# Rounded parts for the latent up-projections, index scores grouped by width, paired score blocks, and a two-piece load of x in a kernel of two transformer blocks

## The reference

```python
q = (_rmsnorm(cq, qa_g) @ w_uq).reshape(B, S, H, MLA_NOPE + MLA_ROPE)
kv = (_rmsnorm(ckv, kva_g) @ w_ukv).reshape(B, S, H, MLA_NOPE + MLA_V)
...
score = jax.nn.relu(jnp.einsum('bqhd,bkd->bqhk', qi, kidx).astype(jnp.float32))
index = jnp.einsum('bqh,bqhk->bqk', wi, score) * idx_scale
```

## Time and profile before

| | |
|---|---|
| three runs | 1757.21, 1757.62, 1757.74 us; median 1757.62 |
| the profiled execution | 1759.74 us, of which the span from the first to the last instruction is 1757.9 |
| granted TensorE clock, mean | 0.998 |
| PE busy | 1749.2 us of the span |
| DVE, ACT, POOL busy | 1032.4, 757.8, 421.5 us |

### The profile page before, as it was taken

The page is one execution under the profiler, slowest core; times in us unless marked ns, Lnnn a source line. Parts: engine busy times, 40 slices in busy tenths (PEclk is TensorE's granted clock), DMA queues, the critical chain, the costliest instruction groups (busy, mean ns, idle before and its releaser), DMA issues.

```text
span 1757.9 us, 25383 instructions
## 1 busy us (share of the span) xinstructions
PE 1749.2 (100%) x9298; PEld 1435.9 (82%) x9298; DVE 1032.4 (59%) x2170; ACT 757.8 (43%) x1396; POOL 421.5 (24%) x326
## 2 busy tenths in 40 slices
PE   9999999999999999999999999999999999999998
PEld 7778878777887888888888888889888888888887
DVE  4888776688877665555433455445756655555333
ACT  6466644546564523233233455556434322222222
POOL 4545553454644500000000332330200200000000
PEclk9999999999999999999999999999999999999999
DMA  6432123323212343333333422223322333333332
GB/s 192 129 100 73 49 65 93 96 68 105 73 49 73 103 132 96 98 96 98 102 108 103 155 61 84 85 84 109 96 73 61 91 100 97 95 95 95 102 103 94
DMA packets 54421, 166.18 MB, mean 95 GB/s; under 512 B 10200, under 2 KB 10712, under 8 KB 54328
## 3 DMA queue, kind: packets, MB, share of 16 engines
q1 hardware_dynamic: 53032, 162.12, 30.6%
q10 hardware_dynamic: 1296, 2.84, 0.5%
HBM read 162.25 MB, written 2.17 MB: 94 GB/s over the span
## 4 chain that ended last, share of the span: by engine, by line
PE 99%; DMA 0%; DVE 0%; ACT 0%; ACTq 0%; POOL 0%; issue 0%; DVEq 0%
PE proj L1113 80%; PE turned L1427 2%; PE o L1449 2%; PE proj L1591 1%; PE proj L1584 1%; PE o L1692 1%; PE o L1792 1%; PE score L1397 1%; PE turned L1079 1%; PE turned L1671 1%; PE score L1781 1%; PE proj L1301 1%; PE turned L1654 1%; PE score L1386 1%; PE score L1654 0%; PE score L1269 0%
## 5 line engine op out<-in xcount | busy, mean ns | idle before, releaser
L1113 PE MATMUL proj<-hhi,whi 128*128 128x512 f32 x1456 | 582.6, 400 | 0.0
L1113 PE MATMUL proj<-hhi,wlo 128*128 128x512 f32 x1456 | 568.4, 390 | 0.0
L1113 PE MATMUL proj<-hlo,whi 128*128 128x512 f32 x1456 | 567.4, 390 | 0.0
L1876 ACT ACTIVATE whi<-ring 128x1024 fp32r<-128x1024 f32 x279 | 295.4, 1059 | 623.7 <-PE proj L1113 602.3
L2384 DVE TENSOR_TENSOR wlo<-ring,whi 128x1024 fp32r<-128x1024 f32 x199 | 243.2, 1222 | 161.2 <-ACT whi L1876 160.7
L1113 PEld LDWEIGHTS proj<-hhi,whi 128*128 128x128 f32 x1456 | 274.0, 188 | 63.6 <-issue 10.4
L1113 PEld LDWEIGHTS proj<-hhi,wlo 128*128 128x128 f32 x1456 | 273.4, 188 | 58.6
L1113 PEld LDWEIGHTS proj<-hlo,whi 128*128 128x128 f32 x1456 | 274.1, 188 | 53.5 <-issue 0.7
L839 POOL TENSOR_TENSOR wlo<-ring,whi 128x512 fp32r<-128x512 f32 x160 | 215.5, 1369 | 339.9 <-ACT whi L1876 339.9
L857 POOL TENSOR_TENSOR prob<-prob 128x512 f32<-128x512 f32 x36 | 56.9, 1581 | 872.2 <-ACT prob L1872 872.2
L1902 ACT ACTIVATE prob<-prob,negmax 128x256 f32<-128x256 f32 (+3 forms) x208 | 114.0, 550 | 74.1 <-DVE negmax L2457 73.4
(11 more groups left out here) (379 smaller groups left out, 2436.9 us busy)
## 6 DMA issues: line engine op xcount, KB each, us to landing
ring<-wstream SPq DMA_DIRECT2D x285, 512.0 KB, 3.6
arena<-lines SPq DMA_DIRECT2D x28, 256.0 KB, 5.7
arena<-x ACTq DMA_DIRECT2D x4, 512.0 KB, 6.3
out<-arena SPq DMA_DIRECT2D x8, 256.0 KB, 2.9
arena<-mem SPq DMA_DIRECT2D x1, 1024.0 KB, 8.5
ring<-wstream SPq DMA_DIRECT2D x12, 64.0 KB, 2.2
ring<-wstream ACTq DMA_DIRECT2D x2, 256.0 KB, 7.7
arena<-rope SPq DMA_DIRECT2D x4, 128.0 KB, 6.4
```

Of the source, the lines that this page charges most:

```text
L1113: mm = pe.matmul(b, rounded(w), rounded(rhs(v, k)), start=(first and n == 0 and p == 0), stop=(last and n == len(blocks) - 1 and p == 2))
L1876: act.activation(rounded(dst), src, ACT.Copy, scale=scale).then_inc(ready, 1)
```

## The change

1. **Up-projections from rounded parts.** UK, UV and UQ become three products of rounded parts like all the others. New work to make the parts: ACT makes high parts of `ckvn`, of the UK and UV weights, of `cqn` (all ahead of `prepare_after("VT0")`), and of the UQ weights (after step 1's exponentials); DVE makes low parts of `ckvn`, UK and UV after `stage_v(0)`; POOL makes the two low parts of `cqn` ahead of the `kA` additions, and those of UQ after UV1. In `TAKE`, UK and UV move ahead of BK1, which goes from slot 11 to slot 13.
2. **Index scores by width.** The four units of a group now have one query block: two groups of 512 columns, two of 384, two of 256. On DVE each accumulation then waits for the one just before it.
3. **C's scores of two blocks at once.** C takes its blocks in the order 0, 2, 3, 1. At steps 24 and 28, `scores` does this step's (128 columns) and the next one's (384) in the same two banks; at steps 25 and 29 it does nothing. `PLAN` moves by a few chunks from step 24 on.
4. **Setup.** x comes in two column pieces of four token parts each; SP issues those of tokens 0 and 2 and slots 0 and 1, ACT those of tokens 1 and 3. Eight warm-up products at first and four more in `first_job`; the four high·high products of the first column piece come ahead of the transposes of the second. The squares of x are summed in two halves; POOL, not ACT, makes slot 1's high part, and the spread of the norm factors comes two chunks later in `second_job`.

The diff, cut to its core:

```diff
-WARM = 12
-X_ORDER = (1, 2, 3, 4, 5, 6, 7, 0)
+WARM = 8
+X_ORDER = (1, 2, 3, 0, 4, 5, 6, 7)
-TAKE = (... "VT0", "BQ1", "BK1", "UK", "UV", "VT1", "UQ", ...
+TAKE = (... "VT0", "BQ1", "UK", "UV", "BK1", "VT1", "UQ", ...
+C_ORDER = (0, 2, 3, 1)
+def double_step(s):
+    return C_STEP <= s < STEPS and s % 4 == 0
 def idx_unit(n):
-    return 4 * (n // (4 * (NQB - 1))) + n % 4, n % (NQB - 1) + 1
+    return n % 8, NQB - 1 - n // 8
...
+            sp.dma_start(ident[:, :], ident_in).then_inc(ident_loaded, 16)
+            for tok in (0, 2):
+                load_x(sp, 0, tok)
+            load_w0(0, w0_loaded)
+            for tok in (0, 2):
+                load_x(sp, 1, tok)
+            load_w0(1, wload[0])
+            sp.dma_start(ring[:, 1, :], wstream[TAKE_FROM[1]]).then_inc(wload[1], 16)
... (pool)
                 after_low(SLOT_OF["BK1"])
                 pool.wait_ge(relu_ready, L * IDX_UNITS + IDX_UNITS)
+                pool.wait_ge(up_out, L * LAYER_UP + 4)
+                for k in range(2):
+                    pool.tensor_tensor(rounded(cqn_lo[:, k, :]), cqn[:, k, :], cqn_hi[:, k, :], ALU.subtract).then_inc(kA_ready, 1)
+                pool.wait_ge(kA_ready, L * LAYER_KA + 2)
                 for h in range(4):
                     pool.tensor_tensor(kA[rows, h, :], krope[rows, 0, :], krope[rows, 1, :], ALU.add).then_inc(kA_ready, 1)
...
                         prepare_after(name)
+                        if name == "UV1":
+                            low_queries()
... (pe, first_job)
+                for _ in range(4):
+                    pe.matmul(b[:, 0:P], ones[:, :], ones[:, :], start=True, stop=True)
+                for n in range(NT):
+                    high_product(n)
                 for n in range(KC + LOW_LAG):
                     if n < KC:
                         k = X_ORDER[n]
+                        if n < NT:
+                            turn_x(1, n)
... (pe, up_k; up_v and up_q alike)
-                    pe.wait_ge(latent_ready, L * 3 + 3)
-                    pe.matmul(b[:, :], w[:, pair * P:(pair + 1) * P], ckvn, start=True, stop=True).then_inc(up_done, 1)
+                    pe.wait_ge(latent_ready, L * LAYER_LATENT + 5)
+                    for p, (w, v) in enumerate(((uk_hi[:, cols], ckvn_hi), (uk_hi[:, cols], ckvn_lo), (wlo[:, slot, cols], ckvn_hi))):
+                        mm = pe.matmul(b[:, :], rounded(w), rounded(v), start=(p == 0), stop=(p == 2))
... (pe, scores)
+                        for t in (s, s + 1) if double_step(s) else (s,):
+                            for p, (q_part, k_part) in enumerate(((q_hi, k_hi), (q_hi, k_lo), (q_lo, k_hi))):
+                                for b in range(2):
+                                    parts(t, b, q_part, k_part, p == 0, p == 2)
... (act)
+                act.wait_ge(latent_ready, L * LAYER_LATENT + 3)
+                high(ckvn, ckvn_hi, up_out)
+                high(raw_loaded("UK")[:, 0:2 * P], uk_hi, up_out)
+                high(raw_loaded("UV")[:, 0:2 * P], uv_hi, up_out)
+                high(cqn, cqn_hi, up_out)
                 prepare_after("VT0")
... (dve)
                 stage_v(0)
+                dve.wait_ge(up_out, L * LAYER_UP + 1)
+                dve.tensor_tensor(rounded(ckvn_lo), ckvn, ckvn_hi, ALU.subtract).then_inc(latent_ready, 1)
+                for n, (name, w_hi) in enumerate((("UK", uk_hi), ("UV", uv_hi))):
+                    slot = SLOT_OF[name] % RING
+                    dve.wait_ge(up_out, L * LAYER_UP + (n + 2))
+                    dve.tensor_tensor(rounded(wlo[:, slot, 0:2 * P]), ring[:, slot, 0:2 * P], w_hi, ALU.subtract).then_inc(latent_ready, 1)
```

More of the change, by code:

```diff
@@ L75 @@
           "DB0", "DB1", "DC0", "DC1", "DH0", "DH1") + tuple(f"OUT{c}" for c in range(KC))
-TAKE = ("QI0", "QI1", "KR", "KI", "CQ0", "CQ1", "CKV", "BQ0", "BK0", "VT0", "BQ1", "BK1", "UK", "UV", "VT1", "UQ",
+TAKE = ("QI0", "QI1", "KR", "KI", "CQ0", "CQ1", "CKV", "BQ0", "BK0", "VT0", "BQ1", "UK", "UV", "BK1", "VT1", "UQ",
         "GT0", "GT1", "GT2", "GT3", "DB0", "VT2", "DB1", "VT3", "SQ0", "SK0", "SQ1", "SK1", "DC0", "DC1",
@@ L90 @@
 SLOT_OF = {name: i for i, name in enumerate(TAKE)}
-SLOT_JOB = [JOB[{"UQ": "UQ2", "UK": "BK1", "UV": "BK1", "KI": "KR"}.get(name, name)] for name in TAKE]
+SLOT_JOB = [JOB[{"UQ": "UQ2", "UK": "BQ1", "UV": "BQ1", "KI": "KR"}.get(name, name)] for name in TAKE]
 RAW = tuple(SLOT_OF[name] for name in ("KI", "UK", "UV", "UQ"))
@@ L878, in _ @@
                     .then_inc((w0_lo, lo_ready)[half], 1)
+            pool.wait_ge(wload[1], 16)
+            for half in range(2):
+                cols = slice(half * SLOT // 2, (half + 1) * SLOT // 2)
+                last_copy = pool.tensor_copy(rounded(whi[:, 1, cols]), ring[:, 1, cols])
+            last_copy.then_inc(hi_ready, 1)
             pool.wait_ge(hi_ready, 2)
@@ L1064, in _, with turn_x @@
             pe.wait_ge(ident_loaded, 16)
-            for tok in range(NT):
-                pe.wait_ge(x_loaded[tok], 16)
-                for c in range(KC):
+            def turn_x(piece, tok):
+                pe.wait_ge(x_loaded[piece][tok], 16)
+                for c in range(4 * piece, 4 * piece + 4):
+                    if c == KC - 1 and tok == 0:
+                        pe.wait_ge(x0_out, 1)
                     mm = pe.transpose(x_bank[c][:, tok * P:(tok + 1) * P], xnat[:, tok, c * P:(c + 1) * P], ident[:, :])
@@ L1070, in _ @@
                         mm.then_inc(xt_done, 1)
+            for tok in range(NT):
+                turn_x(0, tok)
             pe.wait_ge(ones_set, 5)
@@ L1357, in scores @@
                 def scores(s):
-                    if 2 <= s < B_STEPS and s % 2:
+                    if 2 <= s < B_STEPS and s % 2 or after_double(s):
                         return
@@ L1852, in _, with load_x, square_x @@
         def _(act):
[L1853 to L1866 removed]
+            def load_x(piece, tok):
+                cols = slice(piece * S, (piece + 1) * S)
+                act.dma_start(xnat[:, tok, cols], x[tok * P:(tok + 1) * P, cols]).then_inc(x_loaded[piece][tok], 16)
+            for tok in (1, 3):
+                load_x(0, tok)
+            act.dma_start(par[:, :], params[0]).then_inc(par_loaded, 16)
+            act.wait_ge(ones_set, 3)
+            act.activation(negmax[:, :], mhalf[:, 0:4], ACT.Square)
+            for tok in (1, 3):
+                load_x(1, tok)
+            def square_x(tok, half):
+                act.wait_ge(x_loaded[half][tok], 16)
+                act.activation((prob, pT)[half][:, tok, :], xnat[:, tok, half * S:(half + 1) * S], ACT.Square,
+                               accum_out=ms[:, NT * half + tok:NT * half + tok + 1]).then_inc(xsq_ready, 1)
+            for tok in range(NT - 1):
+                square_x(tok, 0)
             def square(n, c):
@@ L1960, in _ @@
                     act.wait_ge(h_ready, KC)
-                    for c in range(4, KC):
+                    for c in (6, 4, 5, 7):
                         act.activation(xT[:, c, :], x_bank[c][:, :], ACT.Copy).then_inc(xt_out2, 1)
```

157 lines of the change are left out of this document (90 added, 67 removed).

## The result

| | before | after |
|---|---|---|
| median of the runs, us | 1757.28 (6 runs) | 1765.01 (6 runs, 1763.57 to 1767.79) |
| profiled execution, us | 1759.74, span 1757.9 | 1763.91, span 1762.1 |
| granted clock, mean of the profiled execution | 0.998 | 0.997 |

The ratio is 1.0041 (95% interval 1.0030 to 1.0051): slower by 0.41%. The prediction was 1754.8 with a range up to 1758.4. It had the wrong sign, and the time lies outside the range.

The account below looks back on a forecast made before the run. PE was taken as the bound, with a product in its pipeline for 1749.2 of 1757.9 us. Wins of 7.4 less lateness of 4.65 gave 2.8 us less: 1754.8 for the runs, range 1751.0 to 1758.4.

Parts of the forecast that it names:

- The step that failed: Index scores: shorter groups win 0.98 us a layer, 1.96 in all, with DVE's serial accumulations hidden behind PE.
- The rival on the clock: Clock falls to its lower level within layer 0's 3 us stall, costing 1.7 us: 1756.5; chance 0.22.
- the layer-0 stall: PE stands still 3.05 us before layer 0's step 1 scores, because BK1's late slot delays POOL's mask and DVE's minima.
- the prediction's own signs of being wrong: No gap at layer 0's `scores(1)`, QI1 moving over 2 us, or a second stretch of granted clock at the lower level.
- Lateness in layers 0 and 1: PE waits for late parts: 3.6 us in layer 0, and 1.05 in layer 1 at VT1, behind POOL's longer list.
- The further 0.55 us at the scores of step 2: Layer 0: step 2's scores use UV0's bank and wait for its later copy, 0.55 us more.
- Up-projections: UK, UV and UQ products on PE get shorter: 1.88 us a layer, 3.8 in all.
- C: C's scores at steps 24 and 28, both layers: one visit of 0.90 replaces 1.20, winning 1.2 us in all.
- the lower bound that I had named: For C's doubled visits: a win of 0, if one visit with twice the instructions saves nothing.
- Setup: Start of the kernel up to QI1's first product: 0.5 us won, between 1.6 won and 0.5 lost.
- S: Setup: start of the last token's transposes of the first column piece, taken as 7.5; QI1 follows at S + 10.55.

Follow-up runs that it names:

- run 11: The run 10 kernel with eight relu buffers instead of four and ACT's square of a latent behind its group's relus: median 1761.59 us, ratio to before 1.0017.
- run 1: The changed kernel with the index units back in their old order, widths mixed, and the accumulation's old wait: median 1760.30 us, ratio to before 1.0008.
- run 5: The kernel before with the index units by width and nothing else of the change: median 1762.35 us, ratio to before 1.0029.
- run 7: The changed kernel with the mask first and POOL's low parts of cqn behind VT1's, index still by width: median 1757.55 us, ratio to before 0.9994.
- run 9: The run 3 kernel, widths mixed, but each accumulation waits for the one right before it: median 1754.57 us, ratio to before 0.9981.
- run 10: The run 7 kernel with the index groups taken 512, 384, 256, 512, 384, 256: median 1752.70 us, ratio to before 0.9968.
- run 2: The changed kernel with POOL's mask of the bias table ahead of BK1's low part: median 1761.80 us, ratio to before 1.0017.
- run 3: The changed kernel with old index order, mask ahead of BK1's low part, and cqn's low parts behind VT1's on POOL: median 1754.70 us, ratio to before 0.9978.
- run 4: The changed kernel with six extra 128x512 subtractions on POOL in layer 0's index stretch: median 1766.43 us, ratio to before 1.0042.
- run 8: The run 7 kernel with eight relu buffers instead of four and ACT's square behind its group's relus: median 1759.33 us, ratio to before 1.0008.
- run 6: The kernel before with the up-projections from rounded parts and nothing else of the change: median 1763.52 us, ratio to before 1.0035.

## Why the prediction was wrong

**The step that failed** is in the paragraph on the index scores: "So it stays hidden; it shows from 0.9 us for one accumulation." The accumulation with its hand-over is 0.85 us, below that threshold, and still it showed. The step compared four accumulations with the distance of one group. It left out what else stands in DVE's list in that stretch: an eviction for each two groups (0.60) and the holding up by POOL, some 0.9 for each accumulation that meets it (1.60 and 1.82 against 0.76). The rows for it stood in the trace of before, in the accumulations' own line (L2568): up to 1.78 us for one beside POOL, and 3.0 us of idle time of DVE ahead of its groups in layer 0. The price was taken from another instruction instead. Two 512-wide groups in a row need about 8 × 0.85 + 0.6 + 1.9 = 9.3 us of DVE (40.34 to 49.42 in the trace, 9.1), and PE brought two in 7.7 before (12 products take 2.94 there, 0.245 each, not 0.227); PE then waits 0.8. The two 384-wide groups behind them, three of whose accumulations meet POOL, need 9.7 with their eviction (49.42 to 59.10), and PE brings two in 7.3 (run 11); PE then waits 2.2. Runs 1, 5 and 7 show that the grouping costs 2.4 to 3.2 us instead of winning 1.96; run 9 that the added wait alone costs about 1; run 10 that with the wide groups apart the loss is gone, though the win is not there either. The shorter groups themselves came as forecast (0.89, 0.72 and 0.56 in run 11, where PE does not wait there).

**The rival on the clock was priced too low.** It had a chance of 0.22 and one fall, 1.7 us. The profile after has a fall right behind the layer-0 stall, as the rival said, and another at SS0 of layer 1; over the runs the clock cost 4.3 us more than before. A second stretch at the lower level was among the prediction's own signs of being wrong. The rival put the fall inside the stall; the trace has it 0.9 us behind its end. The rival also said "a fall in layer 0 was already paid once before, and may shift away". That happened in this trace (0.83 at SS0 before, 1.00 after), but in the mean over runs the falls added up. The Trainium skill (TensorE: Matmul & The Clock Gate, HAM oscillation — how this bites in real kernels) says that a burst behind a long wait starts at half rate. The trace agrees but for the first 0.9 us: UK and UV take 2.44 and 2.09 there, 1.58 and 1.44 at full clock.

**Lateness in layers 0 and 1 was right**: 3.1 for 3.05 and 1.1 for 1.05, each with the named releaser, though layer 0's began 2 us later, behind the index groups. Runs 2 and 3 took them away by the named causes. The further 0.55 us at the scores of step 2 did not come.

**The wins were right in mechanism and too large in size.** Up-projections 3.2 for 3.8: a UK pair takes 1.58, not 1.37, and a UQ 1.40. C 0.6 for 1.2: two blocks in one visit take 1.06, not 0.90; the visit has twice the instructions of the 512-wide group that I took as its likeness, and the win lies about half way between the sum and the lower bound that I had named. Setup 0.25 for 0.5: S was 7.66 (7.5 was taken), QI1 started at 18.48, where S + 10.55 gives 18.21; over the runs the first index group starts anywhere from 38.0 to 39.7, so this term can't be told from no change.

With the index at its real price the sum at full clock would have been −2.8 + 1.96 + 2.5 = +1.7, and with one fall of the clock +3.4: the right sign, but still less than half of what was measured.

## What to carry to other kernels

An engine that is hidden behind PE is checked over the whole stretch, with everything in its list there (evictions, work of a neighbour that holds it up) and with the units in the order in which they come, not for one group at its mean. When a stall of some 2 or 3 us is forecast for PE, the clock's fall belongs into the same sum. A part that saves product time can be late by more than it saves: list what its new pieces stand ahead of on each engine, and move the mark that others wait for (here the mask) to the front of the list first.

## What the runs showed of the hardware

- DVE's accumulation of two SBUF operands, 512 wide, takes 0.76 us alone and 1.34 to 1.82 beside a subtraction on POOL (run 4 and the chain after). The Trainium skill (SBUF — State Buffer, SBUF: two separate sides) calls the port that the two share an exclusive lock, held for the whole instruction; the trace agrees as far as each collision costs DVE 0.6 to 1.1 us, never more than one of POOL's subtractions (some 1.3).
- An instruction of DVE that waits for the mark of the one before it on the same engine starts about 0.09 us behind its end. The wait costs more than that: eight accumulations of mixed width take 8.29 us with it (run 9) and 6.48 without (before).
- The clock: a fall costs 1.7 us where PE has work all the time: 0.17 × 10 at SS0 (before and after) and 0.43 × 4 behind the stall. The mean over the runs is 0.9985 to 0.9995 in the kernels that wait little (before, 3, 9, 10: at most 1.6 us behind the setup), 0.9976 or 0.9977 in four with 4 to 7 us of waits (1, 2, 5, 8), 0.9962 to 0.9966 in four more (after, 4, 6, 11, with 4 to 9 us). Run 7, with 4.5 us, has 0.9987, so the sum of the waits alone does not decide. Why the falls at SS0, where PE waits for nothing, come in some runs and not in others stays open.
